# RWKV loop: transposes of two groups side by side, denser chain inputs and low-rank products, bonus moved behind the chain

## What is computed

```python
def step(S, inp):
    r_t, w_t, k_t, v_t, kk_t, a_t = inp
    S = (S * w_t[:, :, None, :]
         - jnp.einsum('bhvk,bhk->bhv', S, kk_t)[..., None] * (kk_t * a_t)[:, :, None, :]
         + v_t[..., None] * k_t[:, :, None, :])
    return S, jnp.einsum('bhvk,bhk->bhv', S, r_t)
...
lora_w = jnp.einsum('zbtl,zld->zbtd', jnp.tanh(jnp.einsum('btd,zdl->zbtl', xw, w1)), w2)
log_w = -B_DECAY_SCALE * jax.nn.sigmoid((w0[:, None, None, :] + lora_w).astype(f32))
lora_a = jnp.einsum('zbtl,zld->zbtd', jnp.einsum('btd,zdl->zbtl', xa, a1), a2)
a = jax.nn.sigmoid((a0[:, None, None, :] + lora_a).astype(f32))
...
bonus = jnp.sum(jnp.sum(r_h[None] * k_dir * r_k.astype(f32), axis=-1, keepdims=True) * v_h[None], axis=0)
y = y + bonus
```

## Time and profile before

| what | value |
|---|---|
| median of 3 runs | 2890.27 us (2888.03 to 2893.91) |
| the profiled execution | 2888.2 us, span 2886.4 us |
| TensorE matmuls busy | 89% of the span |
| VectorE, ScalarE, GpSimd busy | 43%, 21%, 9% |
| mean granted clock of TensorE | 0.951 |
| chain that ended last | TensorE 80%, VectorE 9%, ScalarE 5%, "issue" 3% |

### The profile page before, as it was taken

The page is one execution under the profiler, slowest core; times in us unless marked ns, Lnnn a source line. Parts: engine busy times, 40 slices in busy tenths (PEclk is TensorE's granted clock), DMA queues, the critical chain, the costliest instruction groups (busy, mean ns, idle before and its releaser), DMA issues.

```text
span 2886.4 us, 63984 instructions
## 1 busy us (share of the span) xinstructions
PE 2571.0 (89%) x28913; PEld 2071.0 (72%) x28913; DVE 1227.2 (43%) x2062; ACT 592.8 (21%) x1032; POOL 255.3 (9%) x162
## 2 busy tenths in 40 slices
PE   6899868999999989968888888888599999999993
PEld 3566545577776757737777777775399999999993
DVE  4434556644554366646666666736200000000004
ACT  2101232200010010024544444431201110111001
POOL 0000230000000000003333221130100000000001
PEclk9999989999999989979999999998799999999996
DMA  7654102312221113310000000002355555655553
GB/s 322 238 232 158 44 2 94 141 64 73 74 90 59 56 59 113 119 43 4 22 22 22 22 22 22 5 6 88 110 199 200 199 205 208 213 187 203 207 196 120
DMA packets 52553, 322.00 MB, mean 112 GB/s; under 512 B 8160, under 2 KB 10336, under 8 KB 21600
## 3 DMA queue, kind: packets, MB, share of 16 engines
q1 hardware_dynamic: 41824, 281.23, 26.7%
q10 hardware_dynamic: 7040, 20.45, 2.0%
q0 software_dynamic: 3456, 16.78, 1.5%
HBM read 289.07 MB, written 29.36 MB: 110 GB/s over the span
## 4 chain that ended last, share of the span: by engine, by line
PE 80%; DVE 9%; ACT 5%; issue 3%; DMA 2%; POOL 1%; SPq 0%; ACTq 0%; POOLq 0%; DVEq 0%
PE PS L868 34%; PE PS L1507 16%; PE PS L1522 8%; PE PS L1123 3%; PE PS L1250 3%; PE PS L846 1%; PE PS L1242 1%; PE PS L1182 1%; PE PS L1314 1%; DMA arena<-in_k 1%; PE PS L596 1%; DVE arena L2481 1%; PE PS L1175 1%; PE PS L1232 1%; DVE ring L2401 1%
## 5 line engine op out<-in xcount | busy, mean ns | idle before, releaser
L868 PE MATMUL PS<-arena,ring 128*128 128x320 f32 x2680 | 753.7, 440 | 41.1 <-DVE arena L2368 12.3
L868 PEld LDWEIGHTS PS<-arena,ring 128*128 128x128 f32 x2680 | 513.9, 193 | 268.4 <-issue 35.2
L1507 PE MATMUL PS<-arena,ring 128*128 128x192 f32 x2816 | 468.6, 330 | 3.1 <-ACT arena L1885 3.1
L1507 PEld LDWEIGHTS PS<-arena,ring 128*128 128x128 f32 x2816 | 466.3, 193 | 4.2 <-ACT arena L1885 4.0
L1522 PE MATMUL PS<-arena,ring 128*128 128x192 f32 x1408 | 230.1, 326 | 0.0
L1522 PEld LDWEIGHTS PS<-arena,ring 128*128 128x128 f32 x1408 | 229.0, 190 | 0.0
L2621 DVE TENSOR_TENSOR arena<-arena,PS 128x192 f32<-128x192 f32 x88 | 31.2, 355 | 441.6 <-ACT arena L1891 441.6
L868 PE MATMUL PS<-arena 128*128 128x320 f32 x536 | 151.1, 432 | 0.0
L1250 PE MATMUL PS<-arena 64*64 64x64 f32 x3200 | 125.2, 227 | 9.7 <-issue 6.6
L868 PEld LDWEIGHTS PS<-arena 128*128 128x128 f32 x536 | 101.8, 190 | 42.4
L787 POOL TENSOR_TENSOR arena<-arena,const 128x512 f32<-128x512 f32 (+1 forms) x24 | 26.3, 1095 | 1110.8 <-DVE arena L2468 777.5
(11 more groups left out here) (332 smaller groups left out, 3201.3 us busy)
## 6 DMA issues: line engine op xcount, KB each, us to landing
ring<-in_k SPq DMA_DIRECT2D x145, 1024.0 KB, 4.8
arena<-in_k SPq DMA_DIRECT2D x48, 1024.0 KB, 9.0
ring<-in_exd SPq DMA_DIRECT2D x32, 1408.0 KB, 5.9
ring<-in_ffd SPq DMA_DIRECT2D x8, 1408.0 KB, 6.1
rkv_s<-arena ACTq DMA_DIRECT2D x24, 320.0 KB, 4.2
expert_rows<-arena POOLq DMA_DIRECT2D x4, 1536.0 KB, 10.2
x<-in_x SPq DMA_DIRECT2D x2, 2560.0 KB, 9.0
arena<-expert_rows ACTq DMA_DIRECT2D x8, 512.0 KB, 4.2
```

Source lines behind the costliest of these rows:

```text
L868: m = pe.matmul(out, lhs[:, k], rhs[:, k], start=k == 0, stop=k == count - 1)
L1507: m = pe.matmul(PS[:, k % 4, t * CAP:(t + 1) * CAP], w[:, kt, t * P:(t + 1) * P], xe[:, kt], start=kt == 0, stop=kt == KT - 1)
```

## The change

- **Transposes**: `double` now makes the new inverses of groups 0 and 1 (`new_inverse`), then the transposes of both in turns (`transposed`), then group 2. So that the two use different combinations of halves, group 0 writes its transpose to the other head side at levels 4 to 32 (`FLIPS`, `side`), group 1 at level 64. Group 1 therefore ends turned, and its Q and MV are written turned.
- **Low-rank products** take 320 tokens of both directions at once, direction 0 from rows 0 to 63 into bank 6, direction 1 from rows 64 to 127 into bank 7; the order is w0, w1, a0, a1, and each is followed by two tanh over 320 tokens.
- **Chain inputs** of both runs are issued in turns, after waiting for both carries.
- **Bonus**: its product, from behind `y_inputs`, goes behind the piece V of the tail; `kds`, `rk`, `rkk` go into the chain (`BONUS_AT`), `yb` behind it.
- **Pieces**: Q is made for groups 0 and 1 together, and the three Q copies go from ScalarE to VectorE. TensorE starts a lap after the last Q copy instead of GB of group 2.

```diff
-PIECES = [(k, i) for i in range(3) for k in ("GK", "GB")] + [("V", 0)] + [(k, i) for i in range(3) for k in ("KB", "Q", "MV")]
-BYACT = ("V", "KB", "Q", "MV")
+PIECES = [(k, i) for i in range(3) for k in ("GK", "GB")] + [("V", 0), ("KB", 0), ("Q", 0), ("Q", 1), ("KB", 1), ("MV", 0), ("MV", 1), ("KB", 2), ("Q", 2), ("MV", 2)]
+BYACT = ("V", "KB", "MV")
+FLIPS = ((4, 8, 16, 32), (64,), ())
+side = lambda i, lv, h: h ^ sum(f < lv for f in FLIPS[i]) % 2
...
+BONUS_AT = {3: "kds", 5: "rk", 6: "rkk"}
...
-                    prep_act.wait(pe, {"a0": "thw0", "w1": "tha0", "a1": "thw1"}[which], j)
-                prep_pe.done(two(6, l2[dd, kind], lhid[dd, kind]), which)
+                    prep_act.wait(pe, {"w1": "thw10", "a0": "thw11", "a1": "tha10"}[which], j)
+                for d in range(2):
+                    m = pe.matmul(PS[:, 6 + d, 0:HT], l2[heads[d], kind], lhid[heads[d], kind, tok], start=True, stop=True)
+                prep_pe.done(m, which)
...
+                if n == 7 and j:
+                    prep_dve.wait(pe, "yb", j)
...
+            def transposed(j, lv, i, r, k):
+                u = PAIRS[i][r][k]
+                for h in range(2):
+                    q = heads[side(i, lv, h)]
+                    m = pe.matmul(PS[heads[side(i, lv + 1, h)], 2 * i + r, k * P + HD:(k + 1) * P], BY[q, u], XX[q, u, 1], start=True, stop=True)
+                return m
+
+            def double(j, lv):
+                new_inverse(j, lv, 0)
+                new_inverse(j, lv, 1)
+                for step in range(2):
+                    if step and lv < 64:
+                        inv_pe.wait(pe, f"X{lv}1", j)
+                    for k in range(4):
+                        m0 = transposed(j, lv, 0, free_first(0, lv) ^ step, k)
+                        m1 = transposed(j, lv, 1, free_first(1, lv) ^ step, k)
+                inv_pe.done(m0, f"Z{lv}0")
+                inv_pe.done(m1, f"Z{lv}1")
+                new_inverse(j, lv, 2)
...
+                if n:
+                    chain_act.wait(pe, f"{ROWS[n - 1][0]}{ROWS[n - 1][2]}", j)
+                    chain_dve.wait(pe, f"{ROWS[n - 1][1]}{ROWS[n - 1][2]}", j)
+                for part in range(2):
                     for h, hs in enumerate(heads):
...
+                        last = []
+                        for q, run in enumerate(runs):
+                            u = RUN[run][t][0]
+                            rhs = Vt[token(u, h), chunk_of(u)] if part == 0 else WU[token(u, h), u, 1]
+                            last += [pe.matmul(PS[hs, 2 + q, 0:HD], KBt[token(u, h), u, part], rhs, start=part == 0, stop=first and part == 1)]
...
-                gram_dve.wait(pe, "GB2", j)
+                gram_dve.wait(pe, "Q2", j)
...
-                if nxt:
-                    bonus(j + 1)
...
+                    if nxt and n == 7:
+                        bonus(j + 1)
...
+                if kind == "Q":
+                    gram_dve.done(dve.tensor_copy(of_pair(QM[:, :, 0], i), bank_pair(piece_bank(n), i, HD)), f"{kind}{i}")
+                    return
...
+                    if nxt and n in BONUS_AT:
+                        bonus_key(j + 1, BONUS_AT[n])
```

More of the change, by code:

```diff
@@ L1126, in lora_mm @@
             def lora_mm(j, which):
-                d, kind = int(which[1]), "wa".index(which[0])
-                dd = slice(64 * d, 64 * d + 64)
+                kind, part = "wa".index(which[0]), int(which[1])
+                tok = (LO, HI)[part]
                 if which == "w0":
@@ L1149, in bonus, with turned @@
                 if j:
-                    post_dve.wait(pe, "RW2", j - 1)
+                    gram_dve.wait(pe, "GB2", j)
                 prep_pe.done(two(6, cst("headones"), T5), "bonus")
+            def turned(j, n, i, k, r):
+                u = PAIRS[i][r][k]
+                for h, hs in enumerate(heads):
+                    m = pe.matmul(PS[heads[side(i, 128, h)], piece_bank(n) + r, k * HD:(k + 1) * HD], QR[hs, u, 0], eye_of(hs), start=True, stop=True)
+                return m
             def piece(j, n):
@@ L1158, in piece @@
                     (gram_act if k0 in BYACT else gram_dve).wait(pe, f"{k0}{i0}", j)
+                elif n and j:
+                    post_dve.wait(pe, "RW2", j - 1)
                 elif n:
@@ L1183, in piece @@
                                               QR[hs, u, 0:2 + j % 2:1 + j % 2], start=True, stop=True)
-                if kind == "Q":
-                    for k in range(len(PAIRS[i][0])):
+                if kind == "Q" and i == 0:
+                    return
+                if kind == "Q" and i == 1:
+                    for k in range(4):
                         for r in range(2):
-                            u = PAIRS[i][r][k]
-                            for hs in heads:
-                                m = pe.matmul(PS[hs, b + r, k * HD:(k + 1) * HD], QR[hs, u, 0], eye_of(hs), start=True, stop=True)
+                            first = turned(j, n - 1, 0, k, r)
+                            m = turned(j, n, 1, k, r)
+                    gram_pe.done(first, "Q0")
+                if kind == "Q" and i == 2:
+                    for k in range(2):
+                        for r in range(2):
+                            m = turned(j, n, 2, k, r)
                 if kind == "MV":
@@ L1251, in double @@
-                inv_pe.done(m, f"Z{lv}{i}")
+                if lv == 64:
+                    return
+                for k in range(len(PAIRS[i][0])):
+                    for r in range(2):
+                        u = PAIRS[i][r][k]
+                        for h in range(2):
+                            q = heads[side(i, lv, h)]
+                            m = pe.matmul(PS[token(u, h), 2 * i + r, k * P:k * P + HD], XX[q, u, 1], BY[q, u], start=True, stop=True)
+                inv_pe.done(m, f"X{lv}{i}")
@@ new lines, in free_first @@
+            def free_first(i, lv):
+                turned_now = side(i, lv, 0)
+                return 1 - turned_now if lv in FLIPS[i] else turned_now
+            def transposed(j, lv, i, r, k):
+                u = PAIRS[i][r][k]
+                for h in range(2):
+                    q = heads[side(i, lv, h)]
+                    m = pe.matmul(PS[heads[side(i, lv + 1, h)], 2 * i + r, k * P + HD:(k + 1) * P], BY[q, u], XX[q, u, 1], start=True, stop=True)
+                return m
+            def double(j, lv):
[4 more added lines that the diff above has]
+                        inv_pe.wait(pe, f"X{lv}1", j)
+                    for k in range(4):
+                        m0 = transposed(j, lv, 0, free_first(0, lv) ^ step, k)
[3 more added lines that the diff above has]
+                new_inverse(j, lv, 2)
+                for step in range(2):
+                    if step and lv < 64:
+                        inv_pe.wait(pe, f"X{lv}2", j)
+                    for k in range(2):
+                        m = transposed(j, lv, 2, free_first(2, lv) ^ step, k)
+                inv_pe.done(m, f"Z{lv}2")
@@ L1320, in y_state @@
                 return m
-            for which in ("w0", "a0", "w1", "a1"):
+            for which in ("w0", "w1", "a0", "a1"):
                 lora_mm(0, which)
@@ L2489, in _ @@
             features(0, 1)
-            bonus_keys(0)
+            for name in ("kds", "rk", "rkk"):
+                bonus_key(0, name)
             bonus(0)
```

108 lines of the change are left out of this document (49 added, 59 removed), and 2 rows, old and new, of the table PREP.

## The result

The changed kernel takes 2905.23 us (median of 5 runs, 2904.76 to 2911.14), the kernel before 2890.2 in the same comparison: ratio 1.0058, 95% interval 1.0043 to 1.0073. It is slower by some 15 us, where 13 less were forecast; the range ended at 2896. The profiled execution is the longest of the five (2911.14 us, span 2909.3); it stands against 2888.2 and 2886.4 of before.

What follows compares the result with a forecast made beforehand. TensorE, busy 89% of the span, was taken as the bound, with instruction supply limiting dense stretches. Seven laps -7.7, lap 7 -1.2, preparation -4.4 and -0.2: -13.5 in all, from 2890.3 to 2877 us; range 2856 to 2896.

Steps and rivals of the forecast that it cites:

- the low-rank products: Ahead of the chain and in lap 0's preparation: pairs on two row halves save 1.9 us a lap, 4.4 in the preparation.
- the tail: End of each lap: 15.75 us instead of 13.65, +2.1, as TensorE waits for the last Q copy; bounds +0.4 and +2.5.
- Rival E: Inversion: two row halves do not share a bank, transposes keep 28 ns, +21 us, 2898; chance 0.03.
- D, the supply: Levels: instruction packets take 3.96 us each, chain starts at 50.4, +2.2 a lap, 2899; chance 0.12.
- it is worth 11 at most: Laps 0 to 6: clock 0.98 means 23 us at 1.2 GHz, worth 11 at most; clock left as it is.
- as much again is 11 us and stays inside the range.: Start of laps: the new wait may bring more time at 1.2 GHz; as much again is 11 us, within the range.
- The chain ends at 16.45.: Chain of each lap: 16.45 us instead of 15.88, +2.2 for bonus operations, 1.6 taken off; bounds -1.6 and +2.2.
- the 1.6 us taken off for denser inputs: Chain inputs: 16 products a row at 16 instead of 28 ns, 0.2 us a row, 8 rows, 1.6 a lap.
- the bound of +2.2: Chain, upper bound: denser inputs bring nothing since they now wait for both carries, +2.2 us a lap.
- The sum: A whole lap: 47.1 + 16.45 + 15.75 = 79.3 us against 80.5, -1.1 a lap, -7.7 over seven laps.
- 7.9 gross: Stretch ahead of the chain: gross saving of 7.9 us a lap, of which 3.8 were expected as gain.
- the forecast's levels: Inversion and solution ahead of the chain: chain starts at 47.1 us instead of 50.9; bounds 45.5 and 50.4.

Runs made afterwards that it cites:

- e2: The changed kernel with the last Q copy on VectorE moved behind `yn`, ahead of `yl` and `yg`; ratio 1.0033 to the kernel before, 2900 us.
- e9: The changed kernel with 3 and 5 unread matmuls a lap in TensorE's waits for Q and between the first low-rank products; ratio 1.0016 to the kernel before, 2895 us.
- e13: The kernel before with 4 unread matmuls in each lap's wait between the first two low-rank products, nothing else changed; ratio 0.9933.
- e3: The kernel before with only the transposes of groups 0 and 1 in turns, one group changing its half; ratio 0.9955, 2877 us.
- e5: The changed kernel with 12 and 14 unread matmuls a lap in the same two TensorE waits, longer than the waits; ratio 1.0151, 2934 us.
- e4: The kernel before with only the chain inputs of both runs in turns, after a wait for both carries; ratio 1.0009, 2893 us.
- e1: The changed kernel with the whole bonus (`kds`, `rk`, `rkk`, product, `yb`) back ahead of the chain; ratio 1.0042 to the kernel before, 2902 us.

## Why the prediction was wrong

Right, by its own steps: the transposes of two groups (16 ns forecast, 14 measured); the waits at the lap's start and for `yb`; more "issue" waits; VectorE as the one that the chain waits for. Right in the number and partly by luck: the low-rank products (17.7 us for 18 by ratio, but 0.8 us a lap for 1.9), and the tail (+2.1 for +2.3 a lap). Of the tail I had all but 0.4 us down to the Q copy: freed of it the tail was to take 14.05, and e2's takes 15.4. The late bonus costs more than I gave it, and the Q copy hid that.

Rival E, the bank shared by two row halves, is refuted by the rows of the inversion. D, the supply, is not what decided: e9 and e13 add instructions and are faster. It was not tested by itself, and the "issue" waits that grew in e3 are a cost that it may explain.

Wrong, against the average lap (82.07 - 1.1 = 81.0 forecast, 85.48 measured, 4.5 us a lap, 32 in all):

- **"it is worth 11 at most", "as much again is 11 us and stays inside the range."** This is the step that failed first. I gave the clock no term, because the laps that I measured by stood at 1.00, and capped its growth at the amount there was. It grew by two and a half times as much: 62 us more at 1.2 GHz. The change adds or lengthens waits (2.58 us for the tanh, 1.2 to 1.6 in the chain, 0.8 to 1.6 at the lap's start), and the work behind such places pays. The part of the miss: 1.6 us a lap ahead of the chain (50.30 for 48.7, and e9 gets 1.9 back by filling) and 1.1 in the chain (19.18 for e5's 18.08 at granted 1.00), 2.7 a lap, 19 us. The Trainium skill (TensorE: Matmul & The Clock Gate, Terms) puts the penalty at half of the time at the lower clock, which makes an estimate of 31 us for the 62. Within one execution the traces have a little less than half: 0.4 us for each us at 1.2 GHz in the chains above, 0.45 ahead of the chain in the kernel before (50.9 us in the two laps without, 54.0 in the two with 6.8). Between executions it is 0.66 in e13 (13.4 for 20) and 0.23 in e9 (10.4 us of laps for 45, its longer tail counted in). So e13 gains more than the clock explains by these rates, and where the rest comes from is open.
- **"The chain ends at 16.45."** At the full clock it is 18.1 (e5, and laps 3 and 5 of the changed kernel): the term for the 2.2 us of bonus operations was right, and they come almost whole on top of 15.9. What was wrong is the 1.6 us taken off for denser inputs. They gain nothing and cost 0.4 (e4: 16.23 to 16.25 in five of seven laps), since the first run's inputs no longer fill the wait for the second's carry. I had this as the bound of +2.2 and did not take it, though the order of the waits in the code said so. 1.6 us a lap, 12 us.
- **The sum.** The parts share what they gain: three dense parts 1.0% by themselves, 0.6% together, for a reason that no run shows. And two late ways in the tail hide each other, so that an edit beside either can't be priced alone.
- Small ones: the preparation gave 2.7 us where I had 4.6, and lap 7 and what follows lost 1.7 where I had a gain of 1.2; the last row of the first windows has lap 7's start at 0.82, where the earlier trace rows had 1.00 in a later stretch of it. The "7.9 gross" ahead of the chain is 8.5 by its own terms (3.9, 1.9 and 2.7); no other number uses it.

Together: 32 + 1.9 + 2.9 us, about the 36 between the 22.9 of the two profiled executions and the -13.5 forecast.

At full clock the forecast's levels hold within 1.3 us: e5's lap 1 takes 50.25 us to the chain, less the 3.7 us by which its added work exceeds the wait 46.5, and e9, nearly all at full clock there, takes 48.4 on the mean, for 47.1 forecast. For the levels, the working fits laps at full clock, and the change left hardly any.

## What to carry to other kernels

Price a wait twice: once by its length, and once by what stands behind it at half clock. Where TensorE is granted less than 1.00 behind a wait, products that nobody reads, cut to that wait's length, are a test of a few lines, and can stay in (0.7% here). Before an interleaving of two operands' work, look whether they come ready at different times: then the order that looks loose is filling a wait. And undo late ways together, not one by one.

## What was not expected of the hardware

Adding work made two kernels faster: the changed one by 0.4% (1.0058 to 1.0016), the kernel before by 0.7%. A wait of 2.6 us with TensorE idle was followed by 6.25 us at 0.50 in which 164 products ran, where 212 and 250 ran at 1.00 with the wait filled (laps 1 and 2). VectorE's `yl` and `yg` took 1.09 and 0.83 us in the changed kernel, where GpSimd was done before `yg`, and 2.10 and 2.04 in e1, beside it.
